# Two request queues re-ordered: a parked FFN half asked for after the second step's output weights, and sample pages asked for one at a time

## The reference, cut to what matters

```python
def swiglu_ffn(x, w_in, w_out):
    g, u = jnp.split(x @ w_in, 2, axis=-1)
    return (jax.nn.silu(g) * u) @ w_out          # D_MODEL 1024, D_FF 2816

def nsa_sample(x, kv_pool, win_cache, page_table, ...):
    past = kv_pool[page_table]                   # 8 samples x 4 pages of 128 rows
    ...
```

## Time and profile before

| | us |
|---|---|
| median of 3 runs | 3842.27 |
| lowest and highest run | 3839.81, 3844.18 |
| the profiled execution | 3833.41 |
| its span, first to last instruction | 3831.8 |
| TensorE busy in the span | 3643.2 (95%) |
| VectorE, ScalarE, GpSimd busy | 2207.3, 1006.2, 1733.0 |
| mean granted TensorE clock | 0.981 of full speed |

### The profile page before, as it was taken

The page is one execution under the profiler, slowest core; times in us unless marked ns, Lnnn a source line. Parts: engine busy times, 40 slices in busy tenths (PEclk is TensorE's granted clock), DMA queues, the critical chain, the costliest instruction groups (busy, mean ns, idle before and its releaser), DMA issues. The chain is left out here.

```text
span 3831.8 us, 53203 instructions
## 1 busy us (share of the span) xinstructions
PE 3643.2 (95%) x19730; PEld 2813.0 (73%) x19730; DVE 2207.3 (58%) x3476; ACT 1006.2 (26%) x2225; POOL 1733.0 (45%) x1501
## 2 busy tenths in 40 slices
PE   8999999998899999989999889989989999999999
PEld 5777777776678888878868656666667788887787
DVE  4666566666356555566642136666655655556566
ACT  3334443334211111100001025556541111111001
POOL 0121111211237998934422126656533399996342
PEclk9999999999799999999999989999999999999999
DMA  4111111111331221252333310000033212115322
GB/s 157 29 45 40 34 40 29 44 40 27 100 105 56 68 76 64 78 186 83 81 113 73 85 40 1 2 1 1 1 114 98 81 52 75 66 57 174 117 76 85
DMA packets 298385, 258.03 MB, mean 67 GB/s; under 512 B 30362, under 2 KB 274195, under 8 KB 296147
## 3 DMA queue, kind: packets, MB, share of 16 engines
q1 hardware_dynamic: 292484, 248.42, 21.1%
q0 software_dynamic: 2048, 5.25, 0.5%
q10 hardware_dynamic: 3650, 1.64, 0.2%
HBM read 208.25 MB, written 51.08 MB: 68 GB/s over the span
## 5 line engine op out<-in xcount | busy, mean ns | idle before, releaser
L1716 PE MATMUL ps<-xn,work 128*128 128x363 f32 (+1 forms) x1536 | 545.2, 473 | 1.3 <-ACT work L1984 1.1
L387 PE MATMUL ps<-work 128*128 128x272 f32 x1676 | 404.9, 398 | 27.6 <-DVE work L475 10.9
L3387 POOL TENSOR_SCALAR work<-work 128x640 f32<-128x640 f32 (+4 forms) x192 | 313.6, 1642 | 196.9 <-DVE work L3288 196.5
L387 PEld LDWEIGHTS ps<-work 128*128 128x128 f32 x1676 | 321.7, 193 | 100.3 <-issue 33.5
L930 PE MATMUL ps<-work 128*128 128x272 f32 x1360 | 367.2, 392 | 0.0
L930 PE MATMUL ps<-xT,work 128*128 128x272 f32 x1280 | 340.6, 394 | 9.2 <-POOL work L1233 9.2
L1716 PEld LDWEIGHTS ps<-xn,work 128*128 128x128 f32 x1536 | 258.6, 190 | 95.0 <-issue 8.6
L930 PE MATMUL ps<-xn,work 128*128 128x272 f32 x1280 | 319.8, 392 | 0.0
L662 POOL TENSOR_TENSOR xT<-xT,work 128x272 f32<-128x272 f32 x96 | 192.4, 2016 | 239.8 <-DVE work L521 156.8
L930 PEld LDWEIGHTS ps<-work 128*128 128x128 f32 x1360 | 258.4, 190 | 53.3
L2447 POOL TENSOR_TENSOR xT<-xT,consts 128x512 f32<-128x512 f32 x96 | 125.6, 1319 | 377.0 <-DVEq L2269 325.3
(11 more groups left out here) (474 smaller groups left out, 6724.8 us busy)
## 6 DMA issues: line engine op xcount, KB each, us to landing
work<-in_ffn_w_in_dram SPq DMA_DIRECT2D x160, 256.0 KB, 3.3
xn<-in_ffn_w_out_dram SPq DMA_DIRECT2D x46, 704.0 KB, 4.7
work<-in_gdn_w_in_dram SPq DMA_DIRECT2D x32, 512.0 KB, 4.2
work<-in_ffn_w_out_dram SPq DMA_DIRECT2D x18, 704.0 KB, 4.7
ffn_parked_hidden_late<-work SPq DMA_DIRECT2D x20, 544.0 KB, 2.9
work<-ffn_parked_hidden_late SPq DMA_DIRECT2D x2, 5440.0 KB, 19.7
ffn_parked_residual<-xT SPq DMA_DIRECT2D x2, 4352.0 KB, 14.0
work<-in_gdn_w_out_dram SPq DMA_DIRECT2D x32, 256.0 KB, 3.0
```

The source lines that it names most:

```text
L387: mm = pe.matmul(acc(n, a), w[:, k, :], t[:, k, :], start=(first and k == 0), stop=(k == hk - 1), skip_group_check=True)
L1716: mm = pe.matmul(unit_acc(u, m), w[j % 2][:, k, :], c.xn[:, k, o:o + cnt], start=(k == 0), stop=(k == KD - 1))
L3387: ins = pool.tensor_scalar(buf(k, g)[:, 0:n], buf(k, g)[:, 0:n], coef[slot(k)][:, g:g + 1], None, ALU.mult)
```

## The change

In `ffn_stages` the wait for all stores and the transfer of `park1` move from the end of `first_back` to the end of `late_back`. `out_stage` calls `late_back` after it has asked for the four weight blocks of step 1. In `prompt_attention` GpSimd no longer asks for 12 pages ahead of its first multiplication. It asks for one page after each of its first 12 "w" steps: all eight of head pair 0 and four of head pair 1. The number of instructions is the same on every engine.

```diff
@@ ffn_stages, first_back and late_back
         sp.dma_start(c.xTf[:, 2 * NT:5 * NT], park[:, 2 * NT:5 * NT]).then_inc(back[1], 16)
         sp.wait_ge(hp, 4 * last + 4)
         sp.dma_start(park1[:, 2 * last:2 * last + 2, :], X(end)).then_inc(late_st, 16)
+
+    def late_back(sp):
+        sp.dma_start(c.xTf[:, 5 * NT:], park[:, 5 * NT:]).then_inc(back[2], 16)
         sp.wait_ge(late_st, 16 * QUADS)
         sp.dma_start(hid3[:, 2:KF, HT:NT], park1).then_inc(late_back_, 16)
-
-    def late_back(sp):
-        sp.dma_start(c.xTf[:, 5 * NT:], park[:, 5 * NT:]).then_inc(back[2], 16)
@@ sample_loads
+    def page(pool, b, n):
+        place = pool.value_load(c.pages[0:1, b * NPG + n:b * NPG + n + 1], min_val=0, max_val=NPHYS - 1)
+        pool.dma_start(d.kv[b][:, n, :], pool_d[ds(place, 1), :, 256:512].rearrange("o p f -> p (o f)")).then_inc(d.kl[b % 3], 16)
+
     def pages(pool, b):
         for n in range(NPG):
-            page = pool.value_load(c.pages[0:1, b * NPG + n:b * NPG + n + 1], min_val=0, max_val=NPHYS - 1)
-            pool.dma_start(d.kv[b][:, n, :], pool_d[ds(page, 1), :, 256:512].rearrange("o p f -> p (o f)")).then_inc(d.kl[b % 3], 16)
+            page(pool, b, n)
@@ prompt_attention, gpsimd
-                for b in range(3):
-                    samples.pages(pool, b)
+                early_pages = [(b, n) for b in range(3) for n in range(NPG)]
                 for k in range(NK):
                     t, kind, i = steps[k]
                     pool.wait_ge(cf, k + 1)
...
                     ins.then_inc(scaled, 1)
+                    if kind == "w" and early_pages:
+                        samples.page(pool, *early_pages.pop(0))
```

More of the change, by code:

```diff
@@ L3020, in sample_loads @@
     win_d = c.io["cache_nsa_win"][0].rearrange("b (n p) k g d -> b p n (k g d)", p=P)
+    def page(pool, b, n):
+        place = pool.value_load(c.pages[0:1, b * NPG + n:b * NPG + n + 1], min_val=0, max_val=NPHYS - 1)
+        pool.dma_start(d.kv[b][:, n, :], pool_d[ds(place, 1), :, 256:512].rearrange("o p f -> p (o f)")).then_inc(d.kl[b % 3], 16)
     def pages(pool, b):
         for n in range(NPG):
-            page = pool.value_load(c.pages[0:1, b * NPG + n:b * NPG + n + 1], min_val=0, max_val=NPHYS - 1)
-            pool.dma_start(d.kv[b][:, n, :], pool_d[ds(page, 1), :, 256:512].rearrange("o p f -> p (o f)")).then_inc(d.kl[b % 3], 16)
+            page(pool, b, n)
     def window(sp, b):
         sp.dma_start(d.wn[b], win_d[b]).then_inc(d.wl[b % 3], 16)
-    d.pages, d.window = pages, window
+    d.page, d.pages, d.window = page, pages, window
     return d
```

## The result

| | before | changed |
|---|---|---|
| median | 3841.04 us (3837.71 to 3844.18) | 3813.44 us (3809.61 to 3818.77) |
| ratio, 95% interval | | 0.9929 [0.9912, 0.9946] |
| the profiled execution, span | 3833.41, 3831.8 us | 3815.72, 3814.0 us |
| mean granted TensorE clock | 0.981 | 0.982 |

The kernel became 27.6 us faster. The two profiled executions differ by only 3833.41 - 3815.72 = 17.7 us. So the question is not only where 19.7 us went, but why the medians say 10 us more than the profiles.

The account below looks back on a forecast made before the run. TensorE, busy 95% of the span, bounds the kernel. Moving `park1` (16.1 us) and the page requests (3.6 us) saves 19.7 us, so 3842.27 - 19.7 = 3822.6 us, range 3817 to 3830 us, chance 0.83.

Parts of the forecast that it names:

- stalls of line 475: FFN output stage, step 1: TensorE's waits for VectorE, 6.50 us in layer 0 and 4.40 in layer 1, would go.
- slow products: Product 2 of step 1, after the stall: 8.33 us in layer 0, 7.66 in layer 1, would take 5.21.
- backlog of `park1`: SP's queue ahead of step 2's weight sum (line 502): moving the queued bytes takes 28.9 us, up to 4.8 more.
- T: The moment in each layer's FFN output stage when SP asks for step 1's last weight block, role 3.
- the 0.4 us that I charged: New TensorE stall before product 2 of step 2, 0.2 us per layer, range 0 to 1.6 us in all.
- A: Stall moves to step 2 of the FFN output stage, line 502 at T + 37; 3835.3 us, chance 0.08.
- C: `park1` moves much more slowly in its new place; slower than before from line 502 at T + 40.2; chance 0.03.
- Rival B: GpSimd's page requests come onto the path in attention, price 13.9 us; 3836.5 us, chance 0.04.
- D: FFN: role 2, step 1's third weight block, stays late for its own reason; only pages count, 3838.7 us, chance 0.02.
- the clock's term: FFN output stages: time saved when product 2 of step 1 runs at 5.21 us, 5.6 us over both layers.
- I take 3.6 us, because the same work follows the restart.: Start of attention: GpSimd's first multiplication comes earlier, 3.6 of TensorE's 5.73 us wait go; range 1.8 to 5.7 us.
- the upper bound of 5.7 us: Start of attention: gain if the rest of TensorE's wait for GpSimd went too.

Follow-up runs that it names:

- park_later: Changed kernel, but `park1` is asked for only after the weights of step 2; 3814.77 us, ratio 0.9936 to the kernel before.
- park_twice: Changed kernel plus a second transfer of the same size, DRAM to DRAM, just ahead of `park1`; 3856.79 us, ratio 1.0043 to the kernel before.
- pages_burst: Changed kernel, but all 12 pages are asked for in one go behind the first "w" step; 3823.14 us, ratio 0.9961 to the kernel before.
- after_again: The changed kernel run again, unchanged; 3814.68 us, ratio 0.9934 to the kernel before.
- before_again: The kernel before run again, unchanged; 3839.87 us, ratio 0.9995 to the kernel before.
- pages_only: Kernel before with only the page requests moved, `park1` at its old place; 3834.39 us, ratio 0.9980 to the kernel before.
- b_plus5: Kernel before plus 5 unread matmuls (2.46 us) in step 2 of layer 0's output stage; ratio 1.0001 to the kernel before.
- b_plus11: Kernel before plus 11 unread matmuls (5.21 us) in step 2 of layer 0's output stage; ratio 1.0036 to the kernel before.
- a_plus5: Changed kernel plus 5 unread matmuls (2.46 us) in step 2 of layer 0's output stage; ratio 0.9962 to the kernel before.
- park_only: Kernel before with only the transfer of `park1` moved, page requests as before; 3821.64 us, ratio 0.9956 to the kernel before.
- keep_warm: Changed kernel plus six unread matmuls before the prompt's attention and four ahead of its first transposes; 3820.08 us, ratio 0.9949 to the kernel before.
- shift5: Changed kernel plus 11 unread matmuls (5.2 us) before product 2 of step 1, layer 0's output stage; 3831.14 us, ratio 0.9978 to the kernel before.
- shift10: Changed kernel plus 21 unread matmuls (9.8 us) before product 2 of step 1, layer 0's output stage; 3829.45 us, ratio 0.9976 to the kernel before.

## Why the prediction was right and wrong

**Right, by its own steps.** The stalls of line 475 are gone in both layers, and the slow products with them: in layer 1, where no other fall lies in the stage, 7.0 us were measured (296.9 - 289.9) and 6.85 forecast. The backlog of `park1` stands before line 502 of step 2, at T + 32.5, inside T + 28.9 to T + 33.7. TensorE did not feel it: product 2 was ready at T + 39.8 and came at T + 40.1 (forecast T + 40.3) without a gap, so the 0.4 us that I charged were not paid; park_later shows the same from the other side. TensorE's wait for GpSimd fell from 5.7 to 2.1 us, the forecast to the tenth, and the requests behind "w" steps were free. Rivals A and C put line 502 at T + 37 and T + 40.2, 4.5 and 7.7 us later than it came; park_twice, at T + 49.5, shows what a longer backlog does. Rival B's price was paid only when the requests stood together, in pages_burst. Against D, role 2 was asked for at 1662.50 and line 502 waited for nothing.

**Wrong: the size. The step that failed is the clock's term, and with it the carrying over to the median.** The sum has one term for the clock, (8.33 - 5.21) + (7.66 - 5.21) = 5.6 us, from one execution, and holds every other fall of the clock in the program fixed; "with 2 us either side for the median" is all the play that it gives them. Measured, the gain in busy time is 0.9, 11.1, 7.6 and 0.1 us in four pairs of traces, where the time standing still is 14.6 to 16.9.

1. "...that execution lies 8.9 us under the median of the runs, so from the median I predict 3842.27 - 19.7 = 3822.6 us." I took the 8.9 us for a constant that the changed kernel has too. They go with the clock: of the 23 executions of the kernel before in the first group, the six under 3840 us had a mean clock of 0.979 or 0.980, the eleven over 3843 us one of 0.976 to 0.978. The six executions of after_again have 0.980 to 0.984. The four of the 23 at 0.980 average 3836.9 us, the seven at 0.977 3844.0 us, so 0.001 of mean clock goes with some 2.4 us. By this estimate the 0.0045 between the two kernels are 11 us; with the 16 us standing still that makes 27 of the 27.6 us measured. Of the 9.2 us between 3822.6 and 3813.44, another 1.2 us are the median of the kernel before itself, which was 3841.04 in the result.

2. "6.50 + (8.33 - 5.21) = 9.62 us in layer 0". The whole stage was 9.8 us shorter, but the price of the stall's own fall was a single sample, and a high one: the product behind the stall took 8.33, 6.89, 7.01, 6.86 and 6.72 us in the traces of before, before_again, pages_only, b_plus5 and b_plus11, so that four times of five its price is 1.5 to 1.8 us and not 3.1. Other falls near the end of the stage, which the sum held fixed, moved the stage's worth to between 6 us (332.7 - 326.7, b_plus5 and a_plus5) and 14 us (335.9 - 322.0, pages_only and park_only).

3. "I take 3.6 us, because the same work follows the restart." Attention became 4.9 us shorter in the first pair of profiles and 5.2 in the second. Of the 4.9 us, 3.8 are standing time less (stretches above: 552.6 - 496.88 = 55.7 us, then 547.7 - 495.74 = 52.0), and 1.1 are matmuls that ran at the higher clock. Half clock in this stage is 36.9, 39.9 and 36.8 us in before, before_again and park_only, and 30.7, 33.4 and 30.7 in after, after_again and pages_only. I had weighed the restart at a bad clock as something that could only take away; that it could also give was in the upper bound of 5.7 us alone, which had another reason.

**Luck.** Against the profiled execution the sum looks good: 3833.41 - 19.7 = 3813.7 us, measured 3815.72. But there 16.9 us came from standing still and 0.9 from the clock, where the sum had 14.1 and 5.6: two misses that nearly cancel. Of the 16.9 us, the three stages of the change hold 14.6; where the other 2.3 us come from was not looked into. With the play of the clock's term as measured, the low end of the range should have lain some 5 us lower.

**Open.** Why the clock falls at the pause near the end of layer 0's output stage in one execution and not in the next. It is not the stall: of five traces with the stall two have this fall (before_again, pages_only), and of those without it keep_warm, a_plus5, shift5 and shift10 have it too. That added matmuls cost more or less than their own time shows that the moment matters, but no run sets the moment at which the clock falls, and why the changed kernel without added work has so high a mean clock is not shown. The Trainium skill, page "TensorE: Matmul & The Clock Gate", section "What's actually happening", says that the gate looks at moments of its own, not tied to the program's start; that the 16 matmuls behind the same pause of 2.75 us take 5.12 us in one execution of the kernel before and 6.81 in another agrees with it.

## What to carry to other kernels

When a large transfer that nobody needs soon stands ahead of small ones in the same queue, ask for it behind them, and compute from the bytes in the queue how late the next small one comes: here it came at T + 32.5, forecast T + 28.9 to T + 33.7. A burst of requests by an engine that others wait for costs its length less the slack (8.2 of 13.9 us here); one at a time, into slack, they were free. And before a sum made from one profiled execution is set against a median, look at how widely the executions of the kernel spread (here 13 us) and give the range that much play. Split a gain into time standing still, which here repeated to 1 or 2 us, and time at a lower clock, which did not: the same change measured 15, 22 or 25 us, depending on moments that nobody chose.

## What the runs showed of the hardware

Adding 2.46 us of matmuls made a kernel of 3.81 ms 6 to 11 us slower, and adding 9.8 us made it no slower than adding 5.2 us. The mean granted clock of all the profiled executions lay between 0.976 and 0.984; a thousandth of it is at most 4 us (7.6 us at half speed, 0.001 x 2 x 3820). A pause of 2.75 us on TensorE was followed by a fall of the granted clock in some executions and not in others, with the matmuls behind it taking 5.12 us or 6.52 to 6.81 us.

`park1` took longer to land in its new place, behind other transfers, than in its old: 23.4 us from asking instead of 19.7 (DMA issues of the changed kernel):

```profile
work<-ffn_parked_hidden_late SPq DMA_DIRECT2D x2, 5440.0 KB, 23.4
```

A page request on GpSimd costs 1.16 us in a row of them (pages_burst: 0.54 us and 0.62 us of issue). Alone, behind a multiplication, the request itself takes 0.59 us instead of 0.54 (median of 12, in the changed kernel and the kernel before). Whether VectorE has a part in these 0.05 us, as the prediction thought possible under rival B, no run shows; in pages_burst, at the same place in the program, it was 0.54 again.
